# Fewer projection matmuls ahead of the sums of squares at three mixer entries, and two GpSimd clears that wait longer

## The chip, the cores and the metric

The kernel runs on one core of a Trainium2 chip. The time is the device time of one execution in microseconds (us). Engines are named as the profile names them: PE is TensorE's matmul, PEld its weight load, DVE is VectorE, ACT ScalarE, POOL GpSimd, SP SyncE (here it only issues loads).

## The reference

256 tokens of width 1024 pass three layers, all in float32. Every stage starts with an RMS norm, so the factor `rsqrt(mean(x*x) + eps)` of each token is needed before the stage's input can be scaled:

```
def rms_norm(x, g):
    y = x * rsqrt(mean(x * x, axis=-1) + EPS)
    return y * g

# layer 1
h = h + 0.5 * swiglu(rms_norm(h, norm_ffn1), ...)
u = rms_norm(h, norm_mix)                    # entry "mix1"
h = h + gated sum of sliding window attention(u) and HGRN2 recurrence(u)
h = h + 0.5 * swiglu(rms_norm(h, norm_ffn2), ...)
h = h + sigmoid(rms_norm(h, norm_ple) @ w_ple_gate) * (p @ w_ple_proj)
h = rms_norm(h, norm_final)
# layer 2, then layer 3
for i in range(2):
    hn = rms_norm(h, attn_norm[i])           # entries "hyb" and "mla"
    h = h + mixer_i(hn)                      # 0: stick breaking + RWKV-7, 1: MLA
    h = h + conv_glu(rms_norm(h, ffn_norm[i]), ...)
    e = rms_norm(p[i] @ ple_w_proj[i], ple_norm[i])
    gate = sigmoid(rms_norm(h, ple_gate_norm[i]) @ ple_w_gate[i])
    h = h + gate * e
h = rms_norm(h, final_norm)
```

The product `p @ ple_w_proj` (256 features of each token into 1024, "the embedding's projection") does not depend on `h`. It can be computed whenever TensorE has time, as long as it is there when the layer ends.

## The kernel before

Activations lie transposed: feature on the partition, token along the row. `h` has 8 tiles of 128 features by 256 tokens. They are worked on in four pairs of tiles, numbered 0 to 3, and the last update of `h` in a stage comes pair by pair.

The program is written by hand, engine by engine. Each engine has one list of instructions in a fixed order, and semaphores tie the lists together. `pe.wait_ge(*folded.at(n))` lets TensorE's list stop until VectorE has finished that event. Nothing behind a waiting instruction overtakes it.

At each mixer's entry the same steps are taken. The names in brackets are the program's, and the lines are those of the profile.

- VectorE updates the four pairs of `h`, and ScalarE squares each (`squares`, L1465).
- At "mix1" and "mla", VectorE adds the squares of pairs 0, 1 and 2 (`folded`, L1983). TensorE sums these and pair 3 over the partitions with one-column matmuls (`add_first_pairs` and `add_last_pair`, both through `add_pair`, L744). At "hyb" TensorE takes all four pairs itself, in `add_weighted_squares` (L771), each as its square arrives.
- VectorE makes the mean (`mean_squares`), GpSimd raises it to the power -1/2 (`rstd`, L1842), VectorE builds two diagonal matrices of the factors (`diagonals`, L2028), and TensorE spreads them over all partitions (`spread`, L780).
- VectorE scales `h` into `xT`, pair by pair (L2038). Then the stage's projections begin (L808 at "mix1" and "hyb", L1352 at "mla").

Between these steps TensorE computes the embedding's projection with `embed(stage, n, b0, pairs)` (L792): four pairs of output tiles, each pair into a PSUM bank of its own, four matmuls a pair. The trace counts a float32 matmul as two instructions, so a pair is x8 there. ScalarE copies each pair out of PSUM (L1590, or L1594 and L1597), and at "mla" all four copies must be out before the stage's first matmul (`embedding_kept`).

GpSimd clears a buffer in two of the stages. At "mix1" it is `AT`, 128 x 1536 floats (L1848), used late in the recurrence. At "hyb" it is one column of `pfT` (L1873). Both are named arena in the profile, since such buffers share one tile.

Of the kernel before, what the change touches and what calls it, by code (L numbers as in the profile page):

```python
# [122 lines left out]
PAIRS = KD // 2  # L123
# [12 lines left out]
def build(nc, I, scratch, out, book):  # L136
    new = {}
    ctx = ExitStack()
    with ctx:
# [3 lines left out]
        def signal(name):  # L143
            return Signal(ctx, nc, name, book, new)
# [200 lines left out]
        h_ready = signal("h_ready")  # L345
        squared = signal("squares_summed")
        mean_ready = signal("mean_squares_ready")
# [13 lines left out]
        x_d = signal("xT_by_vector")  # L361
# [214 lines left out]
        def bay_view(key, offset, shape):  # L576
            b = bay[:, chunks[key] % BAYS, offset:offset + int(np.prod(shape))]
            return b.rearrange("p (a b) -> p a b", a=shape[0]) if len(shape) == 2 else b
# [120 lines left out]
        def _(pe):  # L699
            def weights(key, i=None):  # L700

                c = chunks[key]
                count = 16 * (c // BAYS + 1)
                pe.wait_ge(landed[c % BAYS].sem, count if i is None else i * 16 + count)

            def through(mm, key, i=None):

                if i is None:
                    assert not book or used.count == chunks[key], (key, used.count, chunks[key])
                mm.then_inc(*used.inc(key))  # L710
# [29 lines left out]
            def add_pair(src, q, b):  # L740

                for k in (2 * q, 2 * q + 1):
                    for t in range(TT):
                        mm = nc.tensor.matmul(ps[:, b, t:t + 1], src[:, k, t * P:(t + 1) * P], ones[:, 0:1],  # L744
                                              start=(k + t == 0), stop=(k == KD - 1), skip_group_check=True)
                return mm
# [8 lines left out]
            def add_first_pairs(n, b):  # L755

                pe.wait_ge(*folded.at(n))
                add_pair(sq, 0, b)

            def add_last_pair(n, b):  # L760

                pe.wait_ge(*squared.at(n, PAIRS - 1))
                add_pair(sq, PAIRS - 1, b).then_inc(*sums_p.inc(n))
# [19 lines left out]
            def embed(stage, n, b0, pairs):  # L783

                key = (f"{stage}_proj", 0)
                if 0 in pairs:
                    weights(key)
                w = bay_view(key, 0, [2, D])
                for q in pairs:
                    for j in (2 * q, 2 * q + 1):  # L790
                        for k in range(2):
                            mm = nc.tensor.matmul(ps[:, b0 + q, j % 2 * SEQ:(j % 2 + 1) * SEQ], w[:, k, j * P:(j + 1) * P], pT[:, n, k],  # L792
                                                  start=(k == 0), stop=(k == 1))
                    if q < PAIRS - 1:
                        mm.then_inc(*emb_p.inc(stage, q))
                if PAIRS - 1 in pairs:
                    through(mm, key)
# [147 lines left out]
                    pe.wait_ge(*x_d.at(n, q))  # L945

            def mix1():
                embed("ple1", 0, 4, (0, 1))
                add_first_pairs("mix1", 0)
                add_last_pair("mix1", 0)  # L950
                pe.wait_ge(tab_in.sem, 32)
                pe.wait_ge(*zeros.at("tab"))
                nc.tensor.matmul(ps[0:AH, 3, 0:384], tab[:], hot[:], start=True, stop=True).then_inc(*bias_p.inc("t"))
# [146 lines left out]

            def hyb():
                pe.wait_ge(*rb_ready.at("ple1"))
                embed("ple20", 1, 0, (0, 1))
                pe.wait_ge(*cols_ready.at("block"))
                add_weighted_squares("hyb", 4)
                embed("ple20", 1, 0, (2, 3))
                spread("hyb", 6, 2)
                embedding_kept(pe, "ple20", 0)
                pair_of_features(("wk", 0), 0, first="hyb")
# [219 lines left out]

            def mla():  # L1330
                pe.wait_ge(*rb_ready.at("ple20"))
                embed("ple21", 2, 0, (0, 1))
                add_first_pairs("mla", 4)
                add_last_pair("mla", 4)
                embed("ple21", 2, 0, (2,))
                spread("mla", 5)
                embed("ple21", 2, 0, (3,))
                whole_x("mla")
# [485 lines left out]
        def _(pool):  # L1824
# [18 lines left out]

            def mix1():

                pool.wait_ge(*mean_ready.at("mix1"))
                pool.wait_ge(*bias_p.at("t"))
                nc.gpsimd.memset(AT[:], 0.0).then_inc(*rec_g.inc("zero"))  # L1848
                for n, m in enumerate(LV):

                    z = zT[:, n % 2].rearrange("p a s -> p (a s)").rearrange("p (b m) -> p b m", m=2 * m)
                    b = bT.rearrange("p a s -> p (a s)").rearrange("p (b m) -> p b m", m=2 * m)
                    mid = b[:, :, m - 1:m].to_broadcast([P, RH * SEQ // (2 * m), m])
                    if n == 0:
                        pool.wait_ge(*rec_d.at("sums"))
                    if n >= 2:
                        pool.wait_ge(*rec_p.at("scores", n - 1))
                    nc.gpsimd.tensor_tensor(z[:, :, 0:m], mid, b[:, :, 0:m], ALU.subtract)
                    nc.gpsimd.tensor_tensor(z[:, :, m:2 * m], b[:, :, m:2 * m], mid, ALU.subtract).then_inc(*rec_g.inc("differences", n))
# [9 lines left out]
                    ins.then_inc(*w_lo_g.inc(key))  # L1869

            def hyb():
                pool.wait_ge(*h_ready.at("hyb", PAIRS - 1))
                nc.gpsimd.memset(pfT[:, :, 0:1], 0.0).then_inc(*mix_g.inc("zero"))  # L1873
                for key, tile, tiles, rows in MIXES:
                    pool.wait_ge(*rw_in.at(key))
                    t = slice(tile, tile + tiles)
                    nc.gpsimd.tensor_tensor(xm[0:rows, t], pfT[0:rows, t, 0:SEQ], pfT[0:rows, t, 1:], ALU.subtract).then_inc(*mix_g.inc(key))

                pool.wait_ge(*pre_d.at("bonus"))
                nc.gpsimd.memset(G[:].rearrange("p a b c d -> p (a b c d)"), 0.0).then_inc(*mix_g.inc("G"))  # L1880

                def before(t, *event):

                    for n in range(2):
                        tiles = t[:, n].rearrange("p (b c) -> p b c", b=3)[:, 0::2, :]
                        ins = nc.gpsimd.affine_select(out=tiles, in_=tiles, compare_op=ALU.is_gt, fill=0.0, base=0,
                                                      pattern=[[0, 2], [1, P]], channel_multiplier=-1)
                    ins.then_inc(*stick_g.inc(*event))

                def softplus(g):  # L1890
                    pool.wait_ge(*stick_d.at("softplus", g))
                    before(lsp[:, g % 2], "softplus", g)

                def weights(g):
                    pool.wait_ge(*stick_a.at("weights", g))
                    before(wst[:, g % 2], "weights", g)

                softplus(0)
                softplus(1)
                weights(0)  # L1900
                weights(1)
                softplus(2)
                weights(2)
                softplus(3)
                weights(3)
# [662 lines left out]
```

## Time and profile before

| | |
|---|---|
| median of 3 runs | 1591.19 us (1590.81 to 1591.87) |
| the profiled execution's own time | 1592.14 us |
| its span, first to last instruction | 1590.4 us |
| PE busy | 1499.5 us, 94% of the span |
| PEld busy | 1398.4 us, 88% |
| DVE, ACT, POOL busy | 832.7, 558.9 and 152.0 us |
| mean granted TensorE clock | 0.956 of full speed |

TensorE is busy nearly all the time, so time is lost where it stands still or runs at the lower clock. The three entries lie at about 215, 678 and 1204 us of the span. Times inside the trace are counted from the span's start.

### The profile page before, as it was taken

The page shows a single profiled execution, that of the slowest core. Times are in us where ns is not written, and L with a number is a line of the kernel's source. Part 1 is how long each engine was busy: PE and PEld are TensorE (multiplying, and loading weights), DVE is VectorE, ACT ScalarE, POOL GpSimd, SP SyncE. Part 2 cuts the span into 40 slices and gives each one's busy share as a digit, 9 for nine tenths or more (in the row PEclk, how much of TensorE's full clock was granted, in tenths as well). Part 3 has the DMA queues.
Part 4 walks back from the last instruction along what each step waited for, and adds up shares of the span by engine and source line. Part 5 has one row for each costly group of instructions (what it writes and reads, how often), then busy time and mean ns, then how long its engine had stood idle before and what let it go on. Part 6 is the DMA issues. An engine that isn't in the chain of part 4 may idle for free.

```text
span 1590.4 us, 24781 instructions
## 1 busy us (share of the span) xinstructions
PE 1499.5 (94%) x10432; PEld 1398.4 (88%) x10432; DVE 832.7 (52%) x1130; ACT 558.9 (35%) x689; POOL 152.0 (10%) x149
## 2 busy tenths in 40 slices
PE   5999999899999999999979998999989889999997
PEld 5999998798899999988878878999988468999997
DVE  4666541253256565632664215766674263776765
ACT  3434321123035454421335103443442154444443
POOL 0000000121000000511020000000050032000023
PEclk8999999999999999999989759999999999999998
DMA  8555557533345555433400014455543312455530
GB/s 270 191 185 185 184 153 187 165 106 106 106 159 175 184 183 188 155 99 118 137 25 1 1 53 133 161 184 184 185 159 103 133 53 74 165 185 184 185 133 27
DMA packets 167213, 221.31 MB, mean 139 GB/s; under 512 B 5451, under 2 KB 148036, under 8 KB 167012
## 3 DMA queue, kind: packets, MB, share of 16 engines
q1 hardware_dynamic: 163564, 216.46, 41.2%
q10 hardware_dynamic: 3576, 3.81, 1.3%
q8 instruction: 55, 0.90, 0.2%
q14 instruction: 18, 0.15, 0.0%
HBM read 217.49 MB, written 2.62 MB: 138 GB/s over the span
## 4 chain that ended last, share of the span: by engine, by line
PE 85%; DVE 7%; ACT 4%; issue 2%; POOL 1%; DMA 0%; ACTq 0%; POOLq 0%; SPq 0%; DVEq 0%
PE ps L832 30%; PE ps L868 14%; PE ps L808 12%; PE ps L936 6%; PE ps L918 2%; PE ps L907 2%; PE ps L1231 1%; PE ps L792 1%; DVE x_second_part L1973 1%; PE ps L1352 1%; PE ps L818 1%; PE ps L1368 1%; PE ps L1013 1%; PE ps L1226 1%; PE ps L1380 1%
## 5 line engine op out<-in xcount | busy, mean ns | idle before, releaser
L2053 DVE TENSOR_TENSOR weights_second_parts<-weight_bays,weights_first_parts 128x2048 fp32r<-128x2048 f32 x132 | 302.9, 2302 | 173.5 <-ACT weights_first_parts L1489 173.2
L1489 ACT ACTIVATE weights_first_parts<-weight_bays 128x2048 fp32r<-128x2048 f32 x132 | 252.1, 1918 | 302.8 <-PE ps L832 191.4
L832 PE MATMUL ps<-x_first_part,weights_first_parts 128*128 128x256 f32 x1488 | 211.2, 285 | 1.7 <-DVE weights_second_parts L2053 1.7
L832 PE MATMUL ps<-x_second_part,weights_first_parts 128*128 128x256 f32 x1488 | 208.6, 283 | 0.0
L832 PE MATMUL ps<-x_first_part,weights_second_parts 128*128 128x256 f32 x1488 | 207.3, 282 | 0.0
L808 PE MATMUL ps<-xT,weight_bays 128*128 128x256 f32 (+1 forms) x896 | 197.4, 381 | 1.1 <-DVE xT L2038 1.1
L832 PEld LDWEIGHTS ps<-x_first_part,weights_first_parts 128*128 128x128 f32 x1488 | 192.6, 193 | 2.1 <-ACT weights_first_parts L1489 1.9
L832 PEld LDWEIGHTS ps<-x_second_part,weights_first_parts 128*128 128x128 f32 x1488 | 191.7, 191 | 0.0
L808 PEld LDWEIGHTS ps<-xT,weight_bays 128*128 128x128 f32 (+1 forms) x896 | 168.5, 189 | 26.1 <-ACT embedding L1597 1.3
L832 PEld LDWEIGHTS ps<-x_first_part,weights_second_parts 128*128 128x128 f32 x1488 | 190.6, 191 | 0.0
L868 PE MATMUL ps<-hidden_first_part,weights_first_parts 128*128 128x256 f32 x704 | 141.9, 283 | 5.4 <-ACT weights_first_parts L1489 3.7
L868 PE MATMUL ps<-hidden_second_part,weights_first_parts 128*128 128x256 f32 x704 | 141.9, 283 | 0.0
L868 PE MATMUL ps<-hidden_first_part,weights_second_parts 128*128 128x256 f32 x704 | 139.7, 279 | 0.0
L1868 POOL TENSOR_TENSOR weights_second_parts<-weight_bays,weights_first_parts 128x512 fp32r<-128x512 f32 x48 | 66.7, 1422 | 535.1 <-ACT weights_first_parts L1607 535.1
L868 PEld LDWEIGHTS ps<-hidden_first_part,weights_first_parts 128*128 128x128 f32 x704 | 107.7, 189 | 6.1 <-ACT weights_first_parts L1489 4.0
L868 PEld LDWEIGHTS ps<-hidden_second_part,weights_first_parts 128*128 128x128 f32 x704 | 109.1, 190 | 0.0
L868 PEld LDWEIGHTS ps<-hidden_first_part,weights_second_parts 128*128 128x128 f32 x704 | 108.8, 189 | 0.0
L936 PE MATMUL ps<-arena,weight_bays 128*128 128x256 f32 x320 | 71.6, 386 | 6.5 <-DVE arena L2406 4.5
L936 PEld LDWEIGHTS ps<-arena,weight_bays 128*128 128x128 f32 x320 | 61.7, 194 | 16.0 <-DVE arena L2406 4.7
L1842 POOL TENSOR_TENSOR rstd<-mean_squares,minus_half 128x2 f32<-128x2 f32 (+3 forms) x16 | 14.9, 934 | 562.5 <-DVE mean_squares L2025 426.2
L1526 ACT ACTIVATE arena<-ps 128x512 f32<-128x512 f32 x14 | 8.4, 597 | 121.5 <-PE ps L808 95.0
L1505 ACT ACTIVATE arena<-arena 128x512 f32<-128x512 f32 x22 | 13.9, 633 | 99.9 <-DVE arena L2072 99.9
(369 smaller groups left out, 1882.6 us busy)
## 6 DMA issues: line engine op xcount, KB each, us to landing
weight_bays<-in_w_ffn_in SPq DMA_DIRECT2D x44, 1024.0 KB, 5.2
weight_bays<-in_ffn_w_in SPq DMA_DIRECT2D x44, 1024.0 KB, 5.1
weight_bays<-in_w_ffn_out SPq DMA_DIRECT2D x22, 1024.0 KB, 4.9
weight_bays<-in_ffn_w_out SPq DMA_DIRECT2D x22, 1024.0 KB, 4.9
weight_bays<-in_w_in SPq DMA_DIRECT2D x19, 1024.0 KB, 5.5
weight_bays<-in_hyb_w_in SPq DMA_DIRECT2D x13, 1024.0 KB, 5.2
weight_bays<-in_ple_w_gate SPq DMA_DIRECT2D x8, 1024.0 KB, 4.9
weight_bays<-in_w_out SPq DMA_DIRECT2D x4, 1024.0 KB, 5.0
```

What stands on the lines that cost most here:

```text
L792: mm = nc.tensor.matmul(ps[:, b0 + q, j % 2 * SEQ:(j % 2 + 1) * SEQ], w[:, k, j * P:(j + 1) * P], pT[:, n, k], start=(k == 0), stop=(k == 1))
L808: mm = nc.tensor.matmul(dst, lhs(k), xT[:, k] if rhs is None else rhs(k), start=(k == 0), stop=(k == n - 1), **kw)
L818: nc.tensor.matmul(dst[j], w[:, k, j * P:(j + 1) * P], x_hi[:, k], start=(k == 0 and w is hi and not (one_bank and j)), stop=False, skip_g ...
L832: mm = nc.tensor.matmul(dst, w[:, k, j * P:(j + 1) * P], x[:, k], start=(n + k == 0), stop=(n == 2 and k == KD - 1))
L868: mm = nc.tensor.matmul(ps[:, tile // 2, tile % 2 * SEQ:(tile % 2 + 1) * SEQ], w[:, j, tile * P:(tile + 1) * P], x[:, g % 2, j], start=(g ...
L907: mm = nc.tensor.matmul(ps[:, b, t * width:(t + 1) * width], xT[:, k, t * P:(t + 1) * P], w[:, k, c0:c0 + width], start=(k == 0), stop=(k ...
L918: mm = nc.tensor.matmul(ps[:, b0 + j // 2, j % 2 * SEQ:(j % 2 + 1) * SEQ], w[k // 2][:, k % 2, j * P:(j + 1) * P], srcT[:, k], start=(k == ...
L936: mm = nc.tensor.matmul(ps[:, tile // 2, tile % 2 * SEQ:(tile % 2 + 1) * SEQ], w[:, j, tile * P:(tile + 1) * P], srcT(k) if callable(srcT) ...
L1013: mm = nc.tensor.matmul(o, a, c, start=True, stop=True)
L1489: nc.scalar.activation(hi, raw, ACT.Copy).then_inc(*w_hi_ready.inc(f, g, kind, of - g))
L1868: ins = nc.gpsimd.tensor_tensor(lo[:, part], raw[:, part], hi[:, part], ALU.subtract)
L2053: v.tensor_tensor(lo, raw, hi, ALU.subtract).then_inc(*w_lo_d.inc(f, g, kind, of - g))
```

## The change

TensorE's list is changed at three places, GpSimd's at two. At each of the three entries only pair 0 of the projection stands ahead of the sums of squares, where pairs 0 and 1 stood. Pair 1 is computed right behind the sums. The two clears of GpSimd wait until the last pair of `xT` is scaled: at "mix1" the clear waited for the mean, at "hyb" for the last pair of `h`.

```
             def mix1():
-                embed("ple1", 0, 4, (0, 1))
+                embed("ple1", 0, 4, (0,))
                 add_first_pairs("mix1", 0)
                 add_last_pair("mix1", 0)
+                embed("ple1", 0, 4, (1,))
                 pe.wait_ge(tab_in.sem, 32)
...
             def hyb():
                 pe.wait_ge(*rb_ready.at("ple1"))
-                embed("ple20", 1, 0, (0, 1))
+                embed("ple20", 1, 0, (0,))
                 pe.wait_ge(*cols_ready.at("block"))
                 add_weighted_squares("hyb", 4)
-                embed("ple20", 1, 0, (2, 3))
+                embed("ple20", 1, 0, (1, 2, 3))
                 spread("hyb", 6, 2)
...
             def mla():
                 pe.wait_ge(*rb_ready.at("ple20"))
-                embed("ple21", 2, 0, (0, 1))
+                embed("ple21", 2, 0, (0,))
                 add_first_pairs("mla", 4)
                 add_last_pair("mla", 4)
-                embed("ple21", 2, 0, (2,))
+                embed("ple21", 2, 0, (1, 2))
                 spread("mla", 5)
...
             def mix1():
-                pool.wait_ge(*mean_ready.at("mix1"))
+                pool.wait_ge(*x_d.at("mix1", PAIRS - 1))
                 pool.wait_ge(*bias_p.at("t"))
                 nc.gpsimd.memset(AT[:], 0.0).then_inc(*rec_g.inc("zero"))
...
             def hyb():
-                pool.wait_ge(*h_ready.at("hyb", PAIRS - 1))
+                pool.wait_ge(*x_d.at("hyb", PAIRS - 1))
                 nc.gpsimd.memset(pfT[:, :, 0:1], 0.0).then_inc(*mix_g.inc("zero"))
```

Here is TensorE's list at the entry "mix1" before. L792 is the projection, L744 the sums, L953 one matmul for the attention's bias table, L780 the spread and L808 the stage's first products. The list counts a float32 matmul once.

```order
L792 MATMUL ps<-pT,weight_bays 128x256 x8
L744 MATMUL ps<-ones,squares 128x1 x8
L953 MATMUL ps<-arena,bias_table 8x384
L792 MATMUL ps<-pT,weight_bays 128x256 x4
L780 MATMUL ps<-diagonals,ones 128x128 x2
L792 MATMUL ps<-pT,weight_bays 128x256 x4
```

The same place in the changed kernel, where L954 is the bias table's matmul:

```order
L792 MATMUL ps<-pT,weight_bays 128x256 x4
L744 MATMUL ps<-ones,squares 128x1 x8
L792 MATMUL ps<-pT,weight_bays 128x256 x4
L954 MATMUL ps<-arena,bias_table 8x384
L792 MATMUL ps<-pT,weight_bays 128x256 x4
L780 MATMUL ps<-diagonals,ones 128x128 x2
L792 MATMUL ps<-pT,weight_bays 128x256 x4
```

Four matmuls moved from ahead of the sums to behind them, and so to between the sums and the spread.

TensorE's list at the entry "mla" before, from the projection to the stage's first products (L1352):

```order
L792 MATMUL ps<-pT,weight_bays 128x256 x8
L744 MATMUL ps<-ones,squares 128x1 x8
L792 MATMUL ps<-pT,weight_bays 128x256 x4
L780 MATMUL ps<-diagonals,ones 128x128 x2
L792 MATMUL ps<-pT,weight_bays 128x256 x4
L1352 MATMUL ps<-weight_bays,xT 128x256 x16
```

And in the changed kernel:

```order
L792 MATMUL ps<-pT,weight_bays 128x256 x4
L744 MATMUL ps<-ones,squares 128x1 x8
L792 MATMUL ps<-pT,weight_bays 128x256 x8
L780 MATMUL ps<-diagonals,ones 128x128 x2
L792 MATMUL ps<-pT,weight_bays 128x256 x4
L1353 MATMUL ps<-weight_bays,xT 128x256 x16
```

Here too four matmuls now stand between the sums and the spread. The other engines' lists keep their order. On GpSimd only what the two clears wait for is new.

## Rows read from the trace of the kernel before

**Rows 1.** The page's chain of work that ended last, by engine.

```profile
PE 85%; DVE 7%; ACT 4%; issue 2%; POOL 1%; DMA 0%; ACTq 0%; POOLq 0%; SPq 0%; DVEq 0%
```

**Rows 2.** Timeline at "mix1": start and length in us, engine, line, operation, [idle before].

```profile
215.54 3.33 PEld L792 LDWEIGHTS ps<-pT,weight_bays 128*128 128x128 f32 x16
...
216.46 1.48 DVE L1983 TENSOR_TENSOR squares<-squares 128x512 f32<-128x512 f32 x2
...
218.89 1.97 PEld L744 LDWEIGHTS ps<-ones,squares 128*128 128x128 f32 x16
...
220.88 0.81 PE L953 MATMUL ps<-arena,bias_table 33*8 33x384 f32 x2
...
221.61 2.88 PE L792 MATMUL ps<-pT,weight_bays 128*128 128x256 f32 x8
221.94 1.38 POOL L1848 MEMSET arena<- 128x1536 f32 x1
222.02 1.44 DVE L2028 TENSOR_SCALAR diagonals<-mats,rstd 128x128 f32<-128x128 f32 x2 [0.88 <-POOL rstd L1842]
...
227.29 15.06 PE L808 MATMUL ps<-xT,weight_bays 128*128 128x256 f32 x69
...
235.09 0.74 DVE L2137 TENSOR_SCALAR arena<-arena,one_minus_lower_bound,lower_bound 128x256 f32<-128x256 f32 x2 [5.88 <-ACT arena L1526]
```

**Rows 3.** Windows at "mix1": stretch, busy PE, PEld, DVE, ACT, POOL; clock, DMA share, GB/s.

```profile
222.60:226.00 3.40, 3.40 (x12) 2.86 (x11) 1.48 (x4) 0.60 (x1) 0.72 (x1) 0.50 0.00 0
```

**Rows 4.** Timeline at "hyb", to GpSimd's second clear.

```profile
678.41 3.33 PEld L792 LDWEIGHTS ps<-pT,weight_bays 128*128 128x128 f32 x16
...
681.62 0.63 ACT L1465 ACTIVATE squares<-h 128x512 f32<-128x512 f32 x1 [0.96 <-DVE h L2251]
681.76 3.76 PEld L771 LDWEIGHTS ps<-one_and_squared_gain,squares 128*128 128x128 f32 x32
...
687.78 0.28 DVE L2275 TENSOR_SCALAR diagonals<-mats,rstd 128x128 f32<-128x128 f32 x1
...
690.69 1.05 PE L780 MATMUL ps<-diagonals,ones 128*128 128x128 f32 x8
...
692.87 14.05 PE L808 MATMUL ps<-xT,weight_bays 128*128 128x256 f32 x64 [1.13 <-DVE xT L2038]
...
708.18 0.12 POOL L1873 MEMSET arena<- 128x15 f32 x1
```

**Rows 5.** Windows at "hyb", columns as in the third group.

```profile
686.80:690.20 3.40, 3.40 (x9) 2.71 (x9) 0.87 (x4) 2.66 (x7) 0.35 (x1) 0.50 0.00 0
```

**Rows 6.** Timeline at "mla", from the projection to the stage's first products.

```profile
1204.79 3.33 PEld L792 LDWEIGHTS ps<-pT,weight_bays 128*128 128x128 f32 x16
...
1208.49 0.68 DVE L1983 TENSOR_TENSOR squares<-squares 128x512 f32<-128x512 f32 x1
...
1209.22 1.86 PEld L744 LDWEIGHTS ps<-ones,squares 128*128 128x128 f32 x16 [1.10 <-DVE squares L1983]
...
1211.03 2.40 PE L792 MATMUL ps<-pT,weight_bays 128*128 128x256 f32 x8
...
1212.17 0.48 DVE L2028 TENSOR_SCALAR diagonals<-mats,rstd 128x128 f32<-128x128 f32 x2 [0.81 <-POOL rstd L1842]
...
1214.32 3.22 DVE L2038 SCALAR_TENSOR_TENSOR xT<-h,vector_columns,ps 128x256 f32<-128x256 f32 x8 [1.66 <-PE ps L780]
...
1218.46 7.14 PE L1352 MATMUL ps<-weight_bays,xT 128*128 128x256 f32 x32 [1.61 <-ACT embedding L1597]
```

**Rows 7.** Windows at "mla", columns as in the third group.

```profile
1212.50:1215.80 3.30, 3.30 (x12) 2.76 (x11) 1.64 (x5) 2.52 (x7) 0.00 (x0) 0.50 0.00 0
```

**Rows 8.** Windows further on in the MLA stage, columns as in the third group.

```profile
1239.80:1243.10 3.30, 0.20 (x2) 0.20 (x3) 1.77 (x10) 0.38 (x2) 1.01 (x1) 1.00 0.71 290
1243.20:1249.90 6.70, 4.95 (x14) 3.00 (x13) 2.69 (x8) 0.47 (x1) 0.00 (x0) 0.50 0.00 0
```

**Rows 9.** Timeline near the program's end: one pair's sums at the lower clock.

```profile
1581.87 1.83 PEld L744 LDWEIGHTS ps<-ones,squares 128*128 128x128 f32 x8
```

More of the change, by code:

```diff
@@ L947, in mix1 @@
             def mix1():
-                embed("ple1", 0, 4, (0, 1))
+                embed("ple1", 0, 4, (0,))
                 add_first_pairs("mix1", 0)
                 add_last_pair("mix1", 0)
+                embed("ple1", 0, 4, (1,))
                 pe.wait_ge(tab_in.sem, 32)
@@ L1102, in hyb @@
                 pe.wait_ge(*rb_ready.at("ple1"))
-                embed("ple20", 1, 0, (0, 1))
+                embed("ple20", 1, 0, (0,))
                 pe.wait_ge(*cols_ready.at("block"))
                 add_weighted_squares("hyb", 4)
-                embed("ple20", 1, 0, (2, 3))
+                embed("ple20", 1, 0, (1, 2, 3))
                 spread("hyb", 6, 2)
@@ L1331, in mla @@
                 pe.wait_ge(*rb_ready.at("ple20"))
-                embed("ple21", 2, 0, (0, 1))
+                embed("ple21", 2, 0, (0,))
                 add_first_pairs("mla", 4)
                 add_last_pair("mla", 4)
-                embed("ple21", 2, 0, (2,))
+                embed("ple21", 2, 0, (1, 2))
                 spread("mla", 5)
@@ L1844, in mix1 @@
             def mix1():
-                pool.wait_ge(*mean_ready.at("mix1"))
+                pool.wait_ge(*x_d.at("mix1", PAIRS - 1))
                 pool.wait_ge(*bias_p.at("t"))
@@ L1871, in hyb @@
             def hyb():
-                pool.wait_ge(*h_ready.at("hyb", PAIRS - 1))
+                pool.wait_ge(*x_d.at("hyb", PAIRS - 1))
                 nc.gpsimd.memset(pfT[:, :, 0:1], 0.0).then_inc(*mix_g.inc("zero"))
```

## The prediction

> **What bounds the kernel now.** I read the chain of work that ended last first. TensorE holds 85% of it [rows 1], so at the three entries only one question counts: does TensorE reach the stage's first product sooner or later? I then read the timeline of each entry for TensorE's gaps and for who ends them, and last the windows, for the clock that was granted there. The reader is to see three different cases.
>
> At "mix1" TensorE has no gap. Pairs 0 and 1 of the projection load from 215.54 to 218.87, the sums follow at 218.89, then the bias table, pair 2, the spread, pair 3 and the first product at 227.29 [rows 2]. VectorE had finished folding at 216.46 + 1.48 = 217.94, so the sums stood 0.95 us behind their input. At "hyb" the order is the same without a gap up to the spread; then TensorE waits 1.13 us for the first scaled pair of x [rows 4]. At "mla" TensorE ran out of work ahead of the sums. Its weight loads stop at 1208.12 and the sums start at 1209.22, right behind the fold, which ends at 1209.17. The stage's first product waits again, until 1218.46 [rows 6].
>
> A pair of the projection costs 3.33 / 2 = 1.67 us at the full clock; the three rows with x16 agree [rows 2, 4, 6]. This is the amount that moves at each entry, and nothing is removed from TensorE's list.
>
> **The change at "mix1".** Pair 0 ends at 215.54 + 1.67 = 217.21. The fold is there at 217.94, and at "mla" the sums started 0.05 behind it, so they now start at 217.98. TensorE stands still for 0.77 us that it spent on pair 1. Behind the sums it has pair 1, the bias table and pair 2, as much work as before and 0.77 us later. What the earlier sums buy is an earlier chain to the diagonals. That chain is hidden already. The diagonals were finished at 222.02 + 1.44 = 223.46, while pair 2 kept TensorE until 224.49 [rows 2]. Term: +0.77.
>
> **GpSimd's clear at "mix1".** It ran from 221.94 to 223.32, and the two diagonals beside it took 1.44 us, against 0.48 at "mla" with no clear beside them [rows 2, 6]. Moved behind x, the clear gives these 0.96 us back on VectorE. They lie under pair 2 in this execution and are worth nothing there. With the clock full, pair 2 would end at 221.69 + 1.67 = 223.36, and the diagonals at 223.46 plus about 0.15 to reach TensorE would have held the spread 0.25 us. In the changed order pair 1 stands in between and covers both. I take -0.1, with 0 and -0.25 as ends. The clear now starts about 229. VectorE has its next large work at 235.09, after 5.88 us of waiting [rows 2], so it hides there. If that cover were gone it would cost up to its own 1.38 us. Behind the clear on GpSimd stand the recurrence's differences, which wait for later work of VectorE anyway.
>
> The Trainium skill (SBUF — State Buffer, section "SBUF: two separate sides") says that GpSimd and certain VectorE operations hold one pair of ports by turns, for a whole instruction. The row of 1.44 us agrees. By that rule alone the change would gain the 0.96 us; by the rows, TensorE was not waiting for it.
>
> **The change at "hyb".** Pair 0 ends at 680.08, and the weighted sums start there, not at 681.76. They take 3.76 us for four pairs of squares, 0.94 each, and reach pair 3 at 682.9. Its square is ready at 681.62 + 0.63 = 682.25 [rows 4], and those of the pairs before it come sooner. So no wait arises. Behind the sums TensorE has three pairs instead of two before the spread, the same work in all, so the spread starts when it did. The diagonals, at 688.06, were already ahead of it. Term: 0. GpSimd's second clear takes 0.12 us at 708.18, long after x is scaled, since it stands behind a power that waits for later sums [rows 4]. Its new condition is met long before: 0.
>
> **The change at "mla".** The fold's end, 1209.17, is set by VectorE and ScalarE and does not move. So the sums still start at 1209.22. TensorE now has one pair less ahead of them and stands still from 1206.46 on, 2.7 us instead of about 1. Pair 1 comes behind the sums, ahead of the spread. Was there room? At the full clock pair 2 ends at 1211.03 + 1.67 = 1212.70 and the diagonals at 1212.17 + 0.48 = 1212.65 [rows 6]. Sums to diagonals is just one pair long, so pair 1 comes on top in full: spread, x and the first product all move by 1.67, less 0.1 for the diagonals' way to TensorE that pair 1 covers. The first product waits for all of x and for ScalarE's copy of pair 3, and both hang on the spread, so nothing absorbs the delay. Term: +1.57. The stages behind it are chains that start from TensorE, and pass it on.
>
> **The clock.** Behind the quiet stretches at all three entries (one- and two-column matmuls, gaps) the windows show the granted clock at 0.50, the lower level of 1.2 GHz, for about 3.4 us: from 222.6, 686.8 and 1212.5 [rows 3, 5, 7]. Ahead of each stood 2.0 + 0.8 us of sums and bias table, 3.7 us of sums, and 1 + 1.9 us of gap and sums. Each costs up to 3.4 / 2 = 1.7 us of products. Where TensorE did almost nothing for 3.3 us, the low clock lasted for two such stretches, 6.8 us [rows 8]. What does the change make of it? At "mix1" the quiet time is 0.77 + 1.97, now in one piece, against 2.8 before: I take 0, with ends of -1.7 (the fall does not come) and +1.7 (it lasts twice as long). At "hyb" the sums are as long as before: 0, same ends. At "mla" the quiet time grows from 2.9 to 4.6 us, longer than that of [rows 8]. A fall then comes earlier, lies over the sums as well, and may last twice as long. A pair's sums take 1.83 us at the lower clock [rows 9], so all of them 3.66 instead of 1.86: +1.8. A second stretch over the projection is +1.7, against 1.7 that the fall costs now: at the full clock the spread would start at 1212.80, last 0.53 (half of the x8 in [rows 4]), and 0.04 + 3.22 of scaling and 0.2 to reach TensorE bring the first product to 1216.8, not 1218.46 [rows 6]. The upper end is 1.8 + 1.7 - 1.7 = +1.8, the lower 0. As the gap is longer than the nearest row's, I take +1.2.
>
> The Trainium skill (TensorE: Matmul & The Clock Gate, section "Part 1: The HAM clock gate") says that the array gets the full clock only while it is kept busy. It speaks against this change, which makes gaps. The trace agrees at all three entries. By the rule alone each new gap would be charged with a fall; by the rows a fall is there already each time, and only its length can grow.
>
> **The sum.** +0.77 - 0.1 + 0 + 1.57 + 0 + 1.2 = +3.4 us. From the profiled execution's own 1592.14 us this is 1595.6; the median of the runs shown is 0.95 below that execution, so the forecast for a median is 1591.19 + 3.4, about 1594.6 us.
>
> **The rivals.**
> 1. The clock costs nothing more, or gives some back. For it: the quiet stretches at "mix1" and "hyb" are no longer than before, and at "mix1" they now end sooner, so that one fall may be missed (-1.7). Against it: the gap at "mla". Time: 1591.2 + 2.2, less up to 1.7, so 1591.7 to 1593.4, and to 1593.7 with 0.3 us lost.
> 2. The clock costs more in two places: the full +1.8 at "mla" and +1.7 at "mix1", whose quiet time is in one piece now. Time: 1591.2 + 2.2 + 3.5 = 1596.9, and 1598.6 with "hyb" as well.
> 3. Faster. The mechanism is the sums' chain at "mix1" and "hyb". If TensorE had been waiting there for the diagonals, or if pair 3 and the copies hung on the sums, each entry would give up to the pair's 1.67 us, 3.3 in all, less 1.57 at "mla": 1589.4. It decides only where the diagonals come later than the work ahead of the spread. In the rows they come 1.0 us earlier at "mix1" and 2.6 us earlier at "hyb" (688.06 against a spread at 690.69 [rows 4]). A missed fall at both entries would do as much: 1591.2 + 2.2 - 3.4 = 1590.0.
> 4. The change does not do what it says. The sums do start 0.9 and 1.7 us earlier at two entries, but at "mla" they cannot, since the fold ends when it did. That is already in the sum.
>
> **How the numbers follow.** Between no change and this forecast lie 3.4 us, close to 0.2% of the time (3.2 us), which is about what a measurement of this kernel can tell from no change. The forecast with the clock costing between 0.3 and 3 us, 1593.7 to 1596.4, gets 0.54; rival 1 0.28; rival 2 0.10; the third 0.08. Slower by over 0.2% (above 1594.4) takes most of the forecast's part and all of rival 2: 0.52. Faster by over 0.2% needs both gifts and no cost at "mla": 0.04. Within 0.2%: 0.44. The range leaves out the faster side and the far end of rival 2: 1591.3 to 1598.0.
>
> **What would show it.** After the change the timeline at "mla" should show the sums starting within 0.1 us of the fold, behind a gap of about 2.7 us, and two pairs of the projection, 3.3 us at the full clock, between the sums and the spread. At "mix1" a gap of about 0.8 us should stand ahead of the sums, and the diagonals should take 0.48. At "hyb" there should be no gap, and the distance from the projection's start to the first product should stay at 14.5 us. The forecast is wrong if the first product at "mla" does not come later against the fold than 1218.46 - 1209.17 = 9.3 us, or if the low stretches vanish at an entry.

## The result and the profile after

The changed kernel's median is 1595.14 us (20 runs, 1589.82 to 1595.81), against 1590.89 us for the kernel before in as many runs (1584.38 to 1592.24). The ratio is 1.0031, with a 95% interval of 1.0020 to 1.0042. The ratio compares all runs of both kernels and makes 4.9 us slower (3.2 to 6.7), where the prediction had 3.4. The medians lie 4.25 us apart, and 1595.1 was measured where 1594.6 was forecast.

The profiled execution took 1595.36 us with a span of 1593.6 us, 3.2 us more than before. The first part of its page shows almost the same busy time as before, 1.5 us more on PE:

```profile
PE 1501.0 (94%) x10432; PEld 1397.5 (88%) x10432; DVE 831.8 (52%) x1130; ACT 559.4 (35%) x689; POOL 151.5 (10%) x149
```

So the time has to be looked for at the three entries. First the timeline of the changed kernel at "mix1" (start, length, engine, line, what it waited for), beside [rows 2]:

```profile
215.65 1.60 PEld L792 LDWEIGHTS ps<-pT,weight_bays 128*128 128x128 f32 x8
...
218.10 1.86 PEld L744 LDWEIGHTS ps<-ones,squares 128*128 128x128 f32 x16 [0.86 <-DVE squares L1984]
218.10 1.95 PE L744 MATMUL ps<-ones,squares 128*128 128x1 f32 x16 [0.46 <-DVE squares L1984]
...
221.13 0.48 DVE L2029 TENSOR_SCALAR diagonals<-mats,rstd 128x128 f32<-128x128 f32 x2 [0.88 <-POOL rstd L1843]
...
224.38 0.61 PE L780 MATMUL ps<-diagonals,ones 128*128 128x128 f32 x4
...
226.56 3.62 PE L808 MATMUL ps<-xT,weight_bays 128*128 128x256 f32 x16
...
228.31 1.38 POOL L1849 MEMSET arena<- 128x1536 f32 x1 [7.22 <-DVE xT L2039]
...
228.71 1.00 DVE L2523 TENSOR_SCALAR one_minus_lower_bound<-lower_bound 128x4 f32<-128x4 f32 x1
```

The gap ahead of the sums is there, 0.86 us without a weight load (0.46 us by the matmuls, whose ends are modelled), and the diagonals take 0.48 us. They are ready at 221.61 and the spread starts at 224.38, so they are 2.8 us early. And yet the first product comes 10.9 us behind the start of the projection's loads, 226.56 against 215.65, where it took 11.75 before [rows 2]. The windows of the changed kernel say why. The columns are the stretch, busy PE, PEld, DVE, ACT and POOL, the clock, DMA share and GB/s:

```profile
216.00:226.60 10.60, 10.14 (x55) 8.07 (x54) 4.16 (x10) 2.42 (x4) 0.70 (x1) 1.00 0.30 99
```

The clock stays at 1.00 through the entry. The fall of [rows 3] did not come, which is the -1.7 that the prediction kept as an end. It is also one of the prediction's own signs of being wrong, a low stretch that vanishes at an entry. The last row of the timeline is the moved clear's new neighbour: a VectorE instruction on 128 x 4 numbers takes 1.00 us beside it. The prediction looked only at VectorE's large work, at 235.09 before. The first to use these numbers is that large work, and it still comes after 4.64 us of waiting for ScalarE, so the delay costs nothing.

The same kernel's windows, the first row at "hyb", the second at "mla":

```profile
680.30:686.90 6.60, 6.60 (x21) 5.61 (x21) 1.26 (x7) 2.61 (x6) 1.01 (x1) 0.50 0.02 7
...
1209.30:1216.00 6.70, 6.70 (x21) 5.71 (x22) 0.64 (x3) 2.59 (x6) 0.70 (x1) 0.50 0.01 2
```

Both low stretches are twice as long as those of [rows 5] and [rows 7], and both begin while the sums are running. At "hyb" the timeline of the changed kernel has no gap, as predicted:

```profile
675.73 1.60 PEld L792 LDWEIGHTS ps<-pT,weight_bays 128*128 128x128 f32 x8
...
677.57 4.39 PE L771 MATMUL ps<-one_and_squared_gain,squares 128*128 128x2 f32 x32
681.75 7.68 PEld L792 LDWEIGHTS ps<-pT,weight_bays 128*128 128x128 f32 x24
...
689.66 1.05 PE L780 MATMUL ps<-diagonals,ones 128*128 128x128 f32 x8
...
691.84 3.48 PE L808 MATMUL ps<-xT,weight_bays 128*128 128x256 f32 x15 [1.12 <-DVE xT L2039]
```

The first product comes 16.1 us behind the projection's start, against 14.5 [rows 4], where the prediction expected it to stay. Three pairs at the full clock would load in 5.0 us, and they took 7.68. At "mla":

```profile
1203.91 1.60 PEld L792 LDWEIGHTS ps<-pT,weight_bays 128*128 128x128 f32 x8
...
1207.61 0.68 DVE L1984 TENSOR_TENSOR squares<-squares 128x512 f32<-128x512 f32 x1
...
1208.35 2.65 PEld L744 LDWEIGHTS ps<-ones,squares 128*128 128x128 f32 x16 [2.84 <-DVE squares L1984]
1210.88 5.92 PEld L792 LDWEIGHTS ps<-pT,weight_bays 128*128 128x128 f32 x16
...
1217.03 0.61 PE L780 MATMUL ps<-diagonals,ones 128*128 128x128 f32 x4
...
1221.22 7.14 PE L1353 MATMUL ps<-weight_bays,xT 128*128 128x256 f32 x32 [1.85 <-DVE xT L2039]
```

The sums start 0.06 us behind the fold, after a gap of 2.84 us in the weight loads. The first product comes 1221.22 - 1208.29 = 12.9 us behind the fold's end, against 9.3 [rows 6].

These differences add up to the span. From the projection's first matmul to the first product the three entries give -0.84, +1.64 and +3.65 us, +4.45 together. The stretch between "mix1" and "hyb" is 1.9 us shorter. The kernel before had a low stretch there too, and the changed kernel ran that place at the full clock; first before, then after:

```profile
662.90:666.30 3.40, 3.40 (x18) 3.40 (x17) 2.53 (x2) 0.00 (x0) 3.40 (x4) 0.50 0.00 0
```

```profile
659.50:675.00 15.50, 14.41 (x121) 14.41 (x122) 9.07 (x13) 2.67 (x5) 7.84 (x7) 1.00 0.51 165
```

The other stretches together give +0.7. So 4.45 - 1.9 + 0.7 = 3.2 us. Every large part of this contains a fall of the clock that came, lasted or stayed away. The experiments had to tell which of them belong to the change and which to the one execution that was profiled.

### The profile page after: what moved, and what is told of

Read it like the earlier page. It is cut to its first block, busy times and chain, and to the rows that moved or that the text cites. A ratio compares the mean times of both kernels' runs of the same rounds, so it can differ in the third digit from the quotient of the medians.

```text
span 1593.6 us, 24781 instructions
## 1 busy us (share of the span) xinstructions
PE 1501.0 (94%) x10432; PEld 1397.5 (88%) x10432; DVE 831.8 (52%) x1130; ACT 559.4 (35%) x689; POOL 151.5 (10%) x149
## 4 chain that ended last, share of the span: by engine, by line
PE 84%; DVE 8%; ACT 4%; issue 2%; POOL 1%; DMA 0%; ACTq 0%; POOLq 0%; SPq 0%; DVEq 0%
PE ps L832 30%; PE ps L868 14%; PE ps L808 12%; PE ps L936 6%; PE ps L918 2%; PE ps L907 2%; PE ps L1232 1%; PE ps L792 1%; DVE x_second_part L1974 1%; PE ps L1353 1%; PE ps L818 1%; PE ps L1369 1%; PE ps L1227 1%; PE ps L1381 1%; ACT weights_first_parts L1490 1%
## 5 line engine op out<-in xcount | busy, mean ns | idle before, releaser
L808 PE MATMUL ps<-xT,weight_bays 128*128 128x256 f32 (+1 forms) x896 | 196.6, 379 | 1.1 <-DVE xT L2039 1.1
L808 PEld LDWEIGHTS ps<-xT,weight_bays 128*128 128x128 f32 (+1 forms) x896 | 167.8, 189 | 25.9 <-ACT embedding L1598 1.3
```

The lines of the kernel that those rows point to most:

```text
L808: mm = nc.tensor.matmul(dst, lhs(k), xT[:, k] if rhs is None else rhs(k), start=(k == 0), stop=(k == n - 1), **kw)
```

## The experiments

Theory 1: at "mla" the pair that now stands between the sums and the spread costs 1.6 us, and the gap ahead of the sums brings on a longer low stretch. At "mix1" and "hyb" only the clock matters. Theory 2: the loss is the moved work and the gaps alone. Theory 3: the time went somewhere else, by chance. The results of all kernels are in one table behind the experiments. Distances run from the projection's first matmul to the stage's first product, at "hyb" to the spread.

**1. The edit at "mla" alone.** The kernel before, with this one edit:

```
             def mla():
-                embed("ple21", 2, 0, (0, 1))
+                embed("ple21", 2, 0, (0,))
...
-                embed("ple21", 2, 0, (2,))
+                embed("ple21", 2, 0, (1, 2))
```

> Only the entry of the MLA stage is changed (one pair of the projection ahead of the sums, two behind); the rest is the kernel before. Theory 1 (gap and clock): the distance from the end of VectorE's fold to the stage's first product grows from 9.3 us to 12.5 to 13 us, of which 1.6 is the pair that now stands between the sums and the spread and 1.5 to 2 is a longer stretch at the lower clock; the whole run is 2.5 to 4 us slower than before, which is most of the 4.3 us between the medians. Theory 2 (gap alone): 10.9 us of distance, run 1.6 us slower. Theory 3 (the loss is not at this entry, but falls of the clock that landed elsewhere by chance): distance and run as before.

Measured: 1.0021 (1.0007 to 1.0034), so 3.3 us slower. The timeline at "mla":

```profile
1202.37 2.98 PEld L744 LDWEIGHTS ps<-ones,squares 128*128 128x128 f32 x16 [2.84 <-DVE squares L1983]
...
1205.23 5.57 PEld L792 LDWEIGHTS ps<-pT,weight_bays 128*128 128x128 f32 x16
...
1215.23 1.10 PE L1352 MATMUL ps<-weight_bays,xT 128*128 128x256 f32 x4 [1.85 <-DVE xT L2038]
```

and its windows:

```profile
1203.10:1209.70 6.60, 6.60 (x21) 5.71 (x22) 0.64 (x3) 1.93 (x5) 0.69 (x1) 0.50 0.01 2
```

The first product comes 17.18 us behind the projection's start, as in the whole change (17.20), with the same long low stretch. Theory 1 holds here, and theory 3 falls. This was the fastest of the kernel's 12 runs (1589.24 us, where their median is 1593.78). In it the clock did not fall at the first two entries, which their lists leave as before. "mix1" took 10.14 us and "hyb" 10.48 us to the spread. With one fall they take 11.64 and 12.17. So one fall costs 1.5 to 1.7 us at these entries, and whether it comes is not fixed by the entry's list alone. This is also the execution that shows what the clear is worth at the full clock. VectorE's diagonals, still beside it, hold the spread for 0.31 us:

```profile
222.40 1.44 DVE L2028 TENSOR_SCALAR diagonals<-mats,rstd 128x128 f32<-128x128 f32 x2 [0.88 <-POOL rstd L1842]
...
223.89 0.52 PEld L780 LDWEIGHTS ps<-diagonals,ones 128*128 128x128 f32 x4 [0.31 <-DVE diagonals L2028]
```

**2. TensorE's edit at "mix1" alone.** Pair 1 behind the sums, both clears as before:

```
             def mix1():
-                embed("ple1", 0, 4, (0, 1))
+                embed("ple1", 0, 4, (0,))
                 add_first_pairs("mix1", 0)
                 add_last_pair("mix1", 0)
+                embed("ple1", 0, 4, (1,))
```

> Only TensorE's list at the entry of the first mixer is changed; both clears stay where they were. Theory 1: a gap of 0.8 us ahead of the sums, and no fall of the clock at 222 us, so that the distance from the projection's start to the first product falls from 11.75 to about 10.9 us as in the whole change; the run is 0.5 to 1 us faster. Since pair 1 of the projection covers the diagonals, leaving the clear where it was costs nothing. Theory 2 (gap alone, the clock's fall comes anyway): 12.5 us of distance, run 0.8 us slower.

Measured: 0.9988 (0.9976 to 1.0000), 1.9 us faster at the middle. The entry took 10.79 us, without a fall. The clear did not meet the diagonals, although its condition is the old one. It waits for the bias table's matmul as well, and that now stands behind pair 1. The timeline shows the diagonals done at 221.63, and the clear after them:

```profile
221.15 0.48 DVE L2029 TENSOR_SCALAR diagonals<-mats,rstd 128x128 f32<-128x128 f32 x2 [0.89 <-POOL rstd L1843]
...
222.77 1.38 POOL L1849 MEMSET arena<- 128x1536 f32 x1 [1.65 <-PE ps L954]
```

**3. The edit at "hyb" alone**, taken twice:

```
-                embed("ple20", 1, 0, (0, 1))
+                embed("ple20", 1, 0, (0,))
                 pe.wait_ge(*cols_ready.at("block"))
                 add_weighted_squares("hyb", 4)
-                embed("ple20", 1, 0, (2, 3))
+                embed("ple20", 1, 0, (1, 2, 3))
```

> Only TensorE's list at the entry of the hybrid stage is changed. Theory 1: no gap, but the stretch at the lower clock begins over the sums and lasts 6.8 us where it lasted 3.4, so the distance from the projection's start to the first product grows from 14.5 to about 16.2 us; the run is 1 to 2 us slower. Theory 2 (as the prediction's term had it): the low stretch keeps its length, distance 14.5 us, run as before within 0.3 us.

Measured: 1.0014 (1.0000 to 1.0028), and 13.82 us to the spread, with 6.7 us at the lower clock:

```profile
681.90:688.60 6.70, 6.70 (x21) 5.68 (x21) 1.26 (x7) 2.66 (x6) 1.01 (x1) 0.50 0.04 13
```

The same kernel was profiled once more.

> The kernel with the hybrid stage's edit alone, once more. If the edit makes the low stretch longer, it lasts 6.8 us again and the spread comes 13.8 us behind the projection's start; if that was chance, 12.2 or 10.5 us as in kernels without the edit.

This time it took 12.15 us, with a single low stretch. The long one belongs to some executions only. The run times say how often something slow comes: 7 of this kernel's 12 runs took 1594.0 to 1594.5 us, the profile with the long stretch among them (1594.31), and none of the 90 runs of the kernel before took more than 1592.3. The profile with the short one took 1591.16, and three of the 12 runs 1591.2 to 1591.4.

**4. The two clears alone.** TensorE's lists as before:

```
-                pool.wait_ge(*mean_ready.at("mix1"))
+                pool.wait_ge(*x_d.at("mix1", PAIRS - 1))
...
-                pool.wait_ge(*h_ready.at("hyb", PAIRS - 1))
+                pool.wait_ge(*x_d.at("hyb", PAIRS - 1))
```

> Only GpSimd's two clears wait longer; TensorE's lists are those of before. Both theories: the two diagonals at the first mixer take 0.48 us, not 1.44, and TensorE's first product does not come earlier by more than 0.25 us, because pair 2 of the projection still runs then; the run is the same as before within 0.5 us. If the diagonals had bound TensorE, the first product would come up to 0.96 us earlier.

Measured: 0.9994 (0.9978 to 1.0010), no difference that can be told. The diagonals took 0.48 us and "mix1" 11.63 us, where it took 11.64 with the clear beside them. The 0.96 us are real on VectorE and worth nothing here, in an execution with the fall at this entry.

```profile
221.32 0.48 DVE L2028 TENSOR_SCALAR diagonals<-mats,rstd 128x128 f32<-128x128 f32 x2 [0.88 <-POOL rstd L1842]
...
224.40 0.61 PE L780 MATMUL ps<-diagonals,ones 128*128 128x128 f32 x4
```

**5. The gap at "mla" filled.** The changed kernel, with pair 1 computed once ahead of the sums and a second time behind them. Only the second time tells ScalarE to copy it:

```
-            def embed(stage, n, b0, pairs):
+            def embed(stage, n, b0, pairs, twice=False):
...
-                    if q < PAIRS - 1:
+                    if q < PAIRS - 1 and not (twice and q):
                         mm.then_inc(*emb_p.inc(stage, q))
...
             def mla():
-                embed("ple21", 2, 0, (0,))
+                embed("ple21", 2, 0, (0, 1), twice=True)
```

> The changed kernel, with pair 1 of the projection at the MLA stage's entry computed twice: once ahead of the sums, where it stood, and again behind them. Nothing else of the computation changes. The work behind the sums is that of the change, but TensorE does not stand still for 2.8 us ahead of them. Theory 1 (part of the loss is a longer stretch at the lower clock that the gap brings on): the first product comes 13.7 us behind the projection's start if the clock does not fall, about 15.2 with one fall of 3.4 us, against 17.2 in the changed kernel; the low stretch is 3.4 us or absent, not 6.8. Theory 2 (the loss is in what stands between sums and first product, and the gap has no part in it): 17.2 us as in the changed kernel.

The list of work behind the sums is exactly that of the change. The timeline at "mla":

```profile
1209.09 1.86 PEld L744 LDWEIGHTS ps<-ones,squares 128*128 128x128 f32 x16 [1.11 <-DVE squares L1984]
...
1210.87 3.33 PEld L792 LDWEIGHTS ps<-pT,weight_bays 128*128 128x128 f32 x16
...
1214.44 0.61 PE L780 MATMUL ps<-diagonals,ones 128*128 128x128 f32 x4
...
1218.62 7.14 PE L1353 MATMUL ps<-weight_bays,xT 128*128 128x256 f32 x32 [1.85 <-DVE xT L2039]
```

and its windows, up to the sums' end and from there to the first product:

```profile
1204.60:1211.00 6.40, 5.69 (x36) 4.92 (x36) 3.71 (x6) 1.78 (x3) 0.00 (x0) 1.00 0.40 125
1211.00:1218.60 7.60, 5.77 (x29) 4.81 (x29) 4.16 (x12) 5.30 (x12) 0.70 (x1) 1.00 0.09 9
```

TensorE does one pair more than in the changed kernel and reaches the first product after 13.85 us, not 17.20. The clock stays at 1.00. This decides between the first two theories. Of the distance added, 17.20 - 13.85 = 3.35 us are the gap's, by way of the clock, and 13.85 - 12.13 = 1.72 us are the pair behind the sums (12.13 is the entry before without a fall, as in most profiles of the table below). It is one profile of this kernel. The run as a whole was 1.0013 (0.9997 to 1.0029), with a median of 1592.14 us, 3.0 below the changed kernel's. That fits, but the two intervals overlap, so the run times alone do not show it.

**6. The whole change without its edit at "mla".** The changed kernel, with `embed("ple21", 2, 0, (0, 1))` and `(2,)` as before.

> The whole change without its edit at the MLA stage's entry. Theory 1: the first mixer's entry takes 10.8 us from the projection's start to the first product (11.65 with a fall of the clock before, 10.14 without one), the hybrid's 12.2 or 13.8, the MLA's 12.1 or 13.6 as before; the run is within 2 us of before, and 3 to 4 us faster than the changed kernel. Theory 3 (the MLA entry is not where the time went): the run is as slow as the changed kernel, 4 us above before.

Measured: 0.9988 (0.9974 to 1.0002), and 12.13 us at "mla". Against the whole change's 1.0031 this entry's edit makes 0.43%, 6.8 us, by the middles of two wide intervals. Of the change, then, everything but the edit at "mla" together costs nothing that can be told.

**7 and 8. The kernel before and the changed kernel once more.**

> The kernel before once more, to see where the clock falls in another execution of the same program. If the falls at the entries belong to the program, this profile repeats them: 11.65 us from the projection's start to the first product at the first mixer, 12.2 us to the spread at the hybrid stage, 13.6 at the MLA stage. If they are partly chance (the MLA entries of four kernels that left it alone took 12.1 us without a fall), the MLA entry takes 12.1 us.

> The changed kernel once more. Theory 1 says that the fall at the MLA stage's entry belongs to the gap and comes in every execution: 17.2 us with a low stretch of 6.8 us, or at least 15 us with one of 3.4. At the first mixer 10.8 us. At the hybrid stage the low stretch was 6.8 us in three of four kernels with this edit: 13.8 us to the spread, or 12.2 if it is chance.

The kernel before took 12.13 us at "mla", and the clock stood at 1.00 all through:

```profile
1202.60:1214.80 12.20, 9.66 (x55) 8.08 (x54) 7.79 (x18) 6.86 (x15) 0.69 (x1) 1.00 0.27 71
```

The changed kernel took 17.16 us with the same long stretch, and 12.16 at "hyb":

```profile
1208.90:1215.70 6.80, 6.80 (x24) 6.17 (x25) 0.64 (x3) 1.33 (x3) 0.70 (x1) 0.50 0.01 2
```

So the fall of [rows 7], on which the prediction built, does not come every time. The table below shows it to be the exception.

**9. The wait ahead of the first product at "mla".** The kernel before. The first product no longer waits for all of x and all four copies, but pair by pair, and for the banks that it writes:

```
-                whole_x("mla")
-                for q in range(PAIRS):
-                    embedding_kept(pe, "ple21", q)
                 for n in range(3):
                     key, width = ("down", n), min(256, 672 - 256 * n)
+                    for q in ((0, 1), (), (2, 3))[n]:
+                        embedding_kept(pe, "ple21", q)
...
                         for k in range(KD):
+                            if n + t == 0 and k % 2 == 0:
+                                pe.wait_ge(*x_d.at("mla", k // 2))
```

> The kernel before, but at the MLA stage's entry the first product waits for the scaled pairs of x one by one and for ScalarE's copies of the banks it writes, no longer for all of x and all four copies. This measures what the wait behind the spread holds. Theory: that wait is the 1.6 us of idle time ahead of the first product (2.2 without a fall of the clock), and all of it is on the path: the distance from the projection's start falls from 12.1 or 13.6 us to about 10.4 or 12 us and the run is 1.5 to 2 us faster. Rival: the copies or x bound the later products as well, and the time comes back before the latent norm: run as before.

Measured: 0.9985 (0.9970 to 1.0000), and 10.11 us against 12.13. In the timeline the product follows pair 3 of the projection without a wait:

```profile
1211.72 1.89 PE L792 MATMUL ps<-pT,weight_bays 128*128 128x256 f32 x8
...
1213.45 7.07 PE L1353 MATMUL ps<-weight_bays,xT 128*128 128x256 f32 x32
```

**10. A version out of the parts.** The kernel before with the edit at "mix1", the two clears, and the waits of 9; "hyb" and "mla" keep pairs 0 and 1 ahead of the sums.

> The kernel before with the change's first-mixer edit and its two clears, and with the MLA stage's first product waiting pair by pair. If the two parts add, the run is 2 to 4 us faster than before, and the first entry takes 10.8 us, the MLA's 10.4 to 12. If the gain at the first mixer was only chance of where the clock falls, 1.5 to 2 us faster.

Measured: 0.9973 (0.9961 to 0.9985), a median of 1585.02 us, 4.3 us faster than before (2.4 to 6.2) and faster than the changed kernel. Here is every profile. The column "mix1 to hyb" is the stretch from the first product at "mix1" to the projection at "hyb", the last one the time of the profiled execution itself:

```
kernel                 mix1   mix1 to   hyb to     mla   ratio to   own time
                                  hyb   spread             before
before                11.64     451.2    12.17   13.55          1    1592.14
before, again         11.64     451.0    12.16   12.13               1591.35
changed               10.80     449.3    13.81   17.20     1.0031    1595.36
changed, again        10.79     451.7    12.16   17.16               1595.47
mla edit alone        10.14     449.3    10.48   17.18     1.0021    1589.24
mix1 edit alone       10.79     449.3    12.17   12.12     0.9988    1589.36
hyb edit alone        11.65     450.8    13.82   12.13     1.0014    1594.31
hyb edit, again       11.64     451.3    12.15   12.13               1591.16
clears alone          11.63     450.8    12.16   12.12     0.9994    1585.49
pair 1 twice (mla)    10.79     451.7    12.16   13.85     1.0013    1592.40
all but mla           10.79     449.3    13.82   12.13     0.9988    1592.76
x by pairs (mla)      11.64     451.1    12.16   10.11     0.9985    1587.41
mix1, clears and x    10.79     449.3    12.16   10.11     0.9973    1584.79
```

## Why the prediction came out as it did

**"mla", +1.57 for the pair behind the sums: right.** With the clock at 1.00 in both, the distance is 13.85 us with the pair there and 12.13 without it, so 1.72 us. The wait was read rightly, and what is above the term is size. From one matmul's start to the next a pair takes 1.73 us (at "hyb" the sums begin 3.45 us behind the projection with two pairs ahead of them and 1.72 with one), not half of a row of loads, and the 0.1 us taken off for the diagonals' way did not show.

**"mla", +1.2 for the clock: the mechanism right, the size too small.** This is the term that was mis-sized. The step that failed is the one that read the fall behind the entry before as a fixture ("by the rows a fall is there already each time, and only its length can grow"). Of nine profiles of kernels with TensorE's old order at this entry, eight had no fall there (two of them with the new waits on x). The prediction had only the ninth. With the edit, a low stretch of 6.6 to 6.8 us was there three times in three. The clock's part is therefore 17.20 - 13.85 = 3.35 us, not 1.2. Even against the one profile with a fall it is 3.65 - 1.72 = 1.9. That was the upper end given, 1.8. Filling the gap (experiment 5) shows it to be the gap's doing: the work behind the sums stayed, and the low stretch went. How much of these 5.1 us at the entry reaches the end of the run is less sure. Behind the first product at "mla" the rest of the run took 371.9 to 372.6 us in nine profiles and 374.8 in four, each of these four with a further low stretch of 3.4 us near 1380 us and with the old order at "mla". The edit alone came out 3.3 us slower (1.1 to 5.4), not 5.1. Four of nine against none of three can still be chance.

**"mix1", +0.77 for the gap: right in kind.** 10.80 us with the gap and no fall, 10.14 without either, make 0.66. That is less than the gap of 0.86 us in the loads, mostly since the spread's wait of 0.31 us for the diagonals is gone with the new order. What was sized wrong is the clock's 0. In the old order a fall stood at this entry in six profiles of seven, in the new order in none of six. By that sign of the prediction's own it was wrong here. Why the new order has no fall is not shown. Each fall is worth 11.64 - 10.14 = 1.5. The edit thus gains 0.85 us in the usual case, -1.5 + 0.66, which is the -1.7 end of the term. The edit alone came out 1.9 us faster (3.8 to 0). The prediction also had no term for what follows the entry. The low stretch near 662 us came in each of the six profiles with a fall at "mix1" and in none of the seven others. By the table's column "mix1 to hyb" the old order takes 450.8 to 451.3 us there with it, and the new order 449.3 in four profiles and 451.7 in two, which had another low stretch near 393 us. On the mean that is 0.9 us in the edit's favour, and 0.85 + 0.9 is near the 1.9 measured.

**The clears, -0.1: right within its ends, at 0.** 0.96 us are given back on VectorE, 0.01 us at the first product. Beside the edit at "mix1" they give nothing at all (10.79 us without them, 10.80 with them), since there the clear comes after the diagonals even with its old condition. At "hyb" nothing moves.

**"hyb", 0: right without the clock, too small with it in some executions.** No profile has a gap ahead of the sums, and the first product follows the same list. With the edit the low stretch was 6.8 us long in three profiles of six, in the old order in none of seven. Six and seven profiles do not settle it alone, but with the edit alone 7 of 12 runs were slower than all 90 of the kernel before. So the edit does cost something in about half of the executions, most likely by the long stretch. The mean for the kernel with this edit alone, +2.2 us (0 to 4.5), is too wide to size it.

**The sum.** The middle values are now +0.66 - 1.5 at "mix1", 0 to +1.65 at "hyb" and +1.72 + 3.35 at "mla", 4.2 to 5.9 us. With the 0.9 us behind "mix1" they are 3.3 to 5.0. Measured were 4.9 (3.2 to 6.7). The predicted 3.4 came from a clock term that was 2.1 too small at "mla" and 1.5 too high at "mix1", errors that partly cancelled. So the mechanism at "mla" was right, and that the number came this close is in part luck. The forecast named the right entry, the right sign and the right two causes. The first rival, that the clock costs nothing more, fell at "mla" and held at "mix1". The third rival fell as to its first mechanism, the diagonals. TensorE waited for them 0.31 us at the full clock beside the clear. At "mla" its loads stood still 0.11 us at most ahead of the spread (1210.40 to 1210.51 in the kernel before, again). The prediction's margin at "mix1" was too wide, though. It counted 1.0 us up to the end of pair 2's matmuls, but in the trace before the spread's weights load earlier, 0.40 us behind the diagonals' end at 223.46:

```profile
223.86 1.19 PEld L780 LDWEIGHTS ps<-diagonals,ones 128*128 128x128 f32 x4
```

Its second mechanism, a missed fall, came at "mix1" alone.

The Trainium skill (TensorE: Matmul & The Clock Gate, section "Part 1: The HAM clock gate") has the array at the full clock only while it is kept busy. The profiles agree where the gap is long: 2.84 us with no weight loads ahead of the sums, and a fall in three of three. At "mix1" they do not follow from it simply, since the order that has a gap is the one without the fall. There and at "hyb" the old order had no gap at all, only one- or two-column matmuls, and the clock fell all the same, so the prediction's "agrees at all three entries" said more than its rows. Nor was each new gap charged with a fall, as the prediction took the rule.

## What to carry to other kernels

Work that depends on nothing is worth most where an engine would otherwise stand still ahead of a known event. Before moving it away from there, read how early its neighbours' input is (0.95 us at one entry here, 1.1 us late at another), since the same edit opened a wait of 0.86 us at the one and made a wait of 1.1 us into 2.84 at the other. A gap on TensorE should be priced with the clock behind it. Here 1.7 us of work moved across an event cost 5.1 us up to the stage's first product, and filling the gap with a second computation of the same pair took 3.3 of them back. And a single profile shows one draw of where the clock falls: take several before a fall is booked as part of the kernel, before or after.

## What the runs showed of the hardware

The runs of one program lie on separate levels. The kernel before had 9 of its 20 runs at 1584.4 to 1585.4 us and 11 at 1590.8 to 1592.2, with nothing between. Of its 70 later runs eight lay between, near 1586.8 and 1589.4. Both profiles of this kernel are from the upper level. The clock makes most of the difference, as far as profiles of two kernels with the same list of TensorE can show it. First the windows of the kernel before from "hyb" to "mla" (span 1590.4 us), then those of the kernel with the clears alone (span 1583.8 us), which runs the same list of TensorE over that stretch:

```profile
690.00:1204.00 514.00, 486.38 (x3269) 449.48 (x3268) 266.48 (x355) 165.73 (x190) 48.01 (x46) 0.92 0.34 111
```

```profile
688.70:1198.00 509.30, 481.69 (x3269) 444.95 (x3268) 266.24 (x355) 165.62 (x191) 48.01 (x46) 0.93 0.34 112
```

The same 3269 matmuls take 486.38 us and 481.69 us of busy PE, and this stretch holds 4.7 of the 6.6 us between the two spans. The spread of 6 us between runs of one program is larger than the effect of the change. It is why each comparison above has an interval of 1.7 to 2.6 us to either side of its middle, and why the distances at the entries were the better measure.
